# Seven gate chunks of 440 columns in place of six of 512 in a two-block model kernel

## What is computed

```python
h = rmsnorm(x, norm_mix_g[l])
proj = h @ w_in[l]                  # 1024 x 5384
(lru_x, lru_gate, m_qk, m_v, m_o, m_i, m_f,
 s_q, s_k, s_v, g_a, g_b, g_c) = jnp.split(proj, split_points, axis=-1)
...
merged = (jax.nn.sigmoid(g_a) * ya + jax.nn.sigmoid(g_b) * yb
          + jax.nn.sigmoid(g_c) * yc)
x = x + merged @ w_o[l]
```

## Time and profile before

| | us |
|---|---|
| median of three runs | 749.79 |
| lowest and highest of the three | 749.12, 750.28 |
| span of the profiled execution | 748.0 |
| busy: PE, PEld | 740.5, 648.8 |
| busy: DVE, ACT, POOL | 523.8, 402.5, 49.7 |

### The profile page before, as it was taken

One profiled execution on the slowest core, in us unless ns is written; L12 is line 12 of the kernel. 1 busy time (PEld: TensorE's weight loads), 2 busy tenths in 40 slices (PEclk: granted clock), 3 DMA queues, 4 the chain that ended last, 5 costly groups with the idle time before them and its releaser, 6 DMA issues.

```text
span 748.0 us, 10384 instructions
## 1 busy us (share of the span) xinstructions
PE 740.5 (99%) x4280; PEld 648.8 (87%) x4280; DVE 523.8 (70%) x612; ACT 402.5 (54%) x509; POOL 49.7 (7%) x71
## 2 busy tenths in 40 slices
PE   9999999999999999999999999999999999999996
PEld 9988888889988888888899898789988988888885
DVE  6788946885766666656779998785758655556564
ACT  6678378544545545444653685673647443454442
POOL 0200002120000000000230200030003000000000
PEclk9999999999999999999999999999999999999999
DMA  9866365555565556666466536365065466555431
GB/s 337 280 224 225 137 237 210 171 171 168 176 219 169 170 171 204 215 203 209 154 218 205 165 117 225 116 235 165 21 212 166 162 221 225 172 199 188 162 123 57
DMA packets 74239, 138.42 MB, mean 185 GB/s; under 512 B 3916, under 2 KB 28368, under 8 KB 74064
## 3 DMA queue, kind: packets, MB, share of 16 engines
q1 hardware_dynamic: 72336, 132.69, 52.9%
q10 hardware_dynamic: 1856, 5.06, 1.9%
HBM read 136.69 MB, written 1.05 MB: 184 GB/s over the span
## 4 chain that ended last, share of the span: by engine, by line
PE 97%; DVE 2%; issue 0%; ACT 0%; DVEq 0%; ACTq 0%
PE wide L2074 70%; PE bank L2074 25%; PE bank L2198 2%; DVE low L1318 0%; DVE arena L1581 0%; ACT arena L723 0%; DVE act_hl L1415 0%; DVE xn L1809 0%; DVE x L1819 0%; DVE arena L1641 0%; DVE arena L1637 0%; DVE hid_l L1646 0%; DVE arena L1643 0%; DVE arena L1627 0%; DVEq L263 0%
## 5 line engine op out<-in xcount | busy, mean ns | idle before, releaser
L1318 DVE TENSOR_TENSOR low<-raw,high 128x2048 fp32r<-128x2048 f32 (+1 forms) x118 | 267.0, 2279 | 106.2 <-ACT high L723 101.5
L723 ACT ACTIVATE high<-raw 128x2048 fp32r<-128x2048 f32 (+3 forms) x134 | 234.7, 1770 | 122.8 <-PE wide L2074 95.9
L2074 PE MATMUL wide<-act_hl,high 128*128 128x256 f32 (+1 forms) x1184 | 241.3, 327 | 0.0
L2074 PEld LDWEIGHTS wide<-act_hl,high 128*128 128x128 f32 x1184 | 198.9, 191 | 18.3 <-issue 0.2
L2074 PE MATMUL wide<-high,act_hl 128*128 128x512 f32 x528 | 170.1, 394 | 0.5 <-DVE arena L1581 0.2
L2074 PE MATMUL wide<-act_hl,low 128*128 128x256 f32 x832 | 161.2, 284 | 0.0
L2074 PEld LDWEIGHTS wide<-act_hl,low 128*128 128x128 f32 x832 | 128.6, 192 | 2.8 <-DVE low L1366 0.2
L2074 PEld LDWEIGHTS wide<-high,act_hl 128*128 128x128 f32 x528 | 99.1, 188 | 23.3 <-issue 1.7
L2074 PE MATMUL wide<-low,act_hl 128*128 128x512 f32 x264 | 103.0, 390 | 0.0
L2074 PE MATMUL bank<-high,hid_l 128*128 128x512 f32 x216 | 84.4, 391 | 0.3 <-DVE hid_l L1646 0.3
L2074 PE MATMUL bank<-low,hid_h 128*128 128x512 f32 x216 | 84.2, 390 | 0.0
(11 more groups left out here) (215 smaller groups left out, 681.1 us busy)
## 6 DMA issues: line engine op xcount, KB each, us to landing
raw<-in_w_ff_dram SPq DMA_DIRECT2D x32, 1024.0 KB, 5.3
raw<-in_w_in_dram SPq DMA_DIRECT2D x27, 1024.0 KB, 5.3
raw<-in_w_ffn_in_dram SPq DMA_DIRECT2D x44, 512.0 KB, 4.9
raw<-in_w_ffn_out_dram SPq DMA_DIRECT2D x11, 1024.0 KB, 6.5
raw<-in_w_xkv_dram SPq DMA_DIRECT2D x8, 1024.0 KB, 5.0
raw<-in_w_o_dram SPq DMA_DIRECT2D x4, 1024.0 KB, 5.1
raw<-in_w_out_dram SPq DMA_DIRECT2D x4, 1024.0 KB, 5.0
raw<-in_w_xq_dram SPq DMA_DIRECT2D x4, 1024.0 KB, 5.2
```

Source lines behind the costliest of these rows:

```text
L723: return act.activation(dst, src, func, **k)
L1318: tt(part(low, g), part(raw, g), f32(part(high, g)), SUB).then_inc(sem.low_by_dve, 1)
L2074: return pe.matmul(dst, lhs, rhs, start=start, stop=stop, skip_group_check=loose)
```

## The change

The gate columns are cut into chunks of 440 columns instead of 512: seven instead of six, the last one of 432. The groups keep their view of 512 columns by four row tiles, of which 440 are loaded, split and used, so a gate group holds 1,760 numbers per partition instead of 2,048, and there are 14 gate groups instead of 12. Each chunk still takes 48 matmuls, of 440 columns. The hand-written places of the mixers' small matmuls stay at the same chunk numbers and row tiles; the seventh chunk stands behind the sixth on every engine, with a wait on `gate_in` of its own.

```diff
+GATES = 7
+GATE_W = 440
...
+def gate_width(c):
+    return min(GATE_W, 3 * D - c * GATE_W)
...
-    for c in range(6):
-        add(("gate", c), win, 0, KD, [(0, 2312 + c * NB, NB)], NB)
+    for c in range(GATES):
+        add(("gate", c), win, 0, KD, [(0, 2312 + c * GATE_W, gate_width(c))], NB)
...
+                n = gate_width(c)
                 for t, b in enumerate(me.pair()):
-                    f(gates[:, t, c * NB:(c + 1) * NB], b[:, :], ACT.Tanh, scale=half_rstd[:, t:t + 1])\
+                    f(gates[:, t, c * GATE_W:c * GATE_W + n], b[:, 0:n], ACT.Tanh, scale=half_rstd[:, t:t + 1])\
...
             ahead_of_half(("gate", 5), 1)
             gate_in(5)
+            ahead_of(("gate", 6), "T")
+            gate_in(6)
             high_of_branch(2)
...
             ahead_of_half(("gate", 5), 1)
+            ahead_of(("gate", 6), "T")
             low_of_branch(2)
...
-                    pe.wait_ge(sem.gate_in, 12)
+                    pe.wait_ge(sem.gate_in, 2 * GATES)
...
-            products(("gate", 3), "T")
+            products(("gate", 3), "T", width=GATE_W)
             pe.wait_ge(sem.gate_in, 6)
-            products(("gate", 4), "T", at={3: sb_sums})
+            products(("gate", 4), "T", width=GATE_W, at={3: sb_sums})
             sb_out()
             pe.wait_ge(sem.gate_in, 8)
-            products(("gate", 5), "T", at={1: rep_mem})
+            products(("gate", 5), "T", width=GATE_W, at={1: rep_mem})
+            pe.wait_ge(sem.gate_in, 10)
+            products(("gate", 6), "T", width=gate_width(6))
```

More of the change, by code:

```diff
@@ L2536, in _ @@
             pe.wait_ge(sem.vo_in, 2)
-            products(("gate", 0), "T")
+            products(("gate", 0), "T", width=GATE_W)
             pe.wait_ge(sem.sqk_in, 2)
-            products(("gate", 1), "T", at={2: mlstm_scores})
+            products(("gate", 1), "T", width=GATE_W, at={2: mlstm_scores})
             mlstm_out()
             pe.wait_ge(sem.gate_in, 2)
-            products(("gate", 2), "T", at={6: mlstm_turn})
+            products(("gate", 2), "T", width=GATE_W, at={6: mlstm_turn})
             sb_scores()
             pe.wait_ge(sem.gate_in, 4)
-            products(("gate", 3), "T")
+            products(("gate", 3), "T", width=GATE_W)
             pe.wait_ge(sem.gate_in, 6)
-            products(("gate", 4), "T", at={3: sb_sums})
+            products(("gate", 4), "T", width=GATE_W, at={3: sb_sums})
             sb_out()
             pe.wait_ge(sem.gate_in, 8)
-            products(("gate", 5), "T", at={1: rep_mem})
+            products(("gate", 5), "T", width=GATE_W, at={1: rep_mem})
+            pe.wait_ge(sem.gate_in, 10)
+            products(("gate", 6), "T", width=gate_width(6))
             pe.wait_ge(sem.act_hl, me.seen("act_hl", 2))
```

## The result

The changed kernel takes 751.34 us (751.13 to 752.13) beside 749.61 for the kernel before: +1.73 us; the ratio of the runs' means is 1.0026 with an interval of 1.0016 to 1.0035. That is inside the range (749.0 to 751.9), but not the forecast: I had put 750.6 and a time within 0.2%, and it is slower by a little more than that, an outcome that I gave 0.20. The profiled execution's span went from 748.0 to 749.6.

A forecast was written before the change was run, and what follows sets the result against it. PE was taken to bound the kernel, busy 99% of the span; 0 for its matmuls plus 0.81 us of new wait took the median of 749.79 to 750.6, range 749.0 to 751.9.

The forecast's parts named there:

- What bounds the kernel: Whole kernel: PE is busy 99% of the span, so only its matmuls' cost or its waits move the time.
- The price of the matmuls: PE's gate matmuls: cost in proportion to columns, 0.443 ns each, so 336 narrower ones take the same 65.28 us: 0.
- The rival of the fixed price: Gate matmuls: 13.3 ns fixed on each costs 0.64 us, plus 0.62 of wait: +1.26, 751.1; chance 0.13.
- The early arrival and its wait: Chunk 2's end to chunk 5's diagonals: PE comes 3.25 us earlier and newly waits 0.81 us in all (0.5 to 1.2).
- The chain's saving: ACT's and DVE's work from chunk 2 to the diagonals gets 1.38 us shorter through smaller gate operations.
- the room: At chunk 5's diagonals before the change: 1.06 us between the second diagonal, hand-over included, and PE's need of it.
- What had cover: mLSTM's transpose, work queued behind the wait, extra operations, loads and the order behind the gates: no new wait expected.
- the mLSTM's transpose: Small PE step in chunk 2: PE comes 4.2 us earlier, DVE 1.2, and about 1.3 us of room stay.
- the swapped banks: The pair of banks that each later chunk takes is swapped, costed at nothing.
- The rival in which the chain doesn't shrink: ACT's and DVE's gate operations cost as before, so the wait is 2.19 us: 752.0; chance 0.12.
- the steps: Gate matmuls take the next multiple of 32 columns: gain 2.56 us, wait 1.64, in sum -0.9, 748.9; chance 0.10.
- No wait: At the diagonals the chain is looser than its rows look, so the change does nothing: 749.8; chance 0.09.

The follow-up runs named there:

- the streams: Behind the changed kernel's last product, streams of 30 matmuls, one width each from 512 to 256 columns: 226.7 ns each at 512, 200.0 at 440, 119.8 at 256.

## Why the prediction came out as it did

**What bounds the kernel** was right: PE throughout, and the whole change is in PE's gate stage.

**The price of the matmuls was the step that failed.** I took it in proportion to the columns, 0.443 ns each, and so 0; it was +1.73 us. The argument was that the first matmul of 256 columns behind wide ones takes 0.11 us, half of what 512 take. The half was a coincidence: there are 6.7 ns above the columns at 256 (113.3 with 64 or 32 stationary columns) and 13.3 at 512, but 13 to 18.5 from 320 to 504. Neither were my bounds wide enough: at 440 the price, 16.7, is outside both ends (11.5 in proportion, 13.3 fixed). Of the 1.73, 48 x 13.3 ns = 0.64 is for the count and the other 1.09 for the width, some 3.3 ns more at each of 288 and 2.8 at each of 48. The rival of the fixed price, 751.1, was right that a matmul has a price beside its columns, and I gave it 0.13; it had that price too low and the wait too high (0.62), so that its sum, 1.26, came nearer than its terms.

**The early arrival and its wait were right in kind.** With the price that was measured, the forecast's own sum is 102 x 26.7 ns = 2.72 early, less 1.38, less 1.06: 0.28 us of wait; the trace has 0.34. I had forecast 0.81 mostly because I thought PE faster than it is. The chain's saving was 1.38 by my terms; from ACT's read of chunk 2 to the second diagonal it took 126.74 - 98.67 = 28.07 us before and 121.08 - 94.43 = 26.65 after, 1.42 less. That 0.28 lies so near 0.34 is partly luck, because I took the room at the second diagonal, and PE stopped for the first. In the trace of before (timeline of DVE) the first one is done at 126.54:

```profile
126.26 0.28 DVE L1374 TENSOR_SCALAR diag<-ident,rstd 128x128 f32<-128x128 f32 x1
```

The room there is 127.77 - 126.54 - 0.06 = 1.17. From the last matmul of chunk 2 to the place of the product PE takes 127.77 - 98.24 = 29.53 us before and 120.72 - 94.03 = 26.69 after, so it is 2.84 early; the 0.12 more than 2.72 are got back behind the small matmuls. 2.84 - 1.42 - 1.17 leaves 0.25 us, for the 0.23 of the trace, and starting again, which I had only among the bounds, adds 0.11. Low parts of 1,760 elements took 1.98 us for 2.0 expected, so rows of 440 out of 512 carry no price of their own. Lengthening the chain, lengthening PE's lead and moving the product all moved the wait by about what the sum says.

**What I had not seen** is the 0.3 us behind the small matmuls, which the matmuls of 440 columns get back. Why they do wasn't tested.

**What had cover** kept it: no wait at the mLSTM's transpose, on a load, or behind the gates, and the swapped banks cost nothing that shows.

**The sum** had one term at nothing that was 1.73, one that was 0.47 too large, and left out the 0.3: 0.81 + 1.73 - 0.47 - 0.3 gives the 1.78 of the trace; the medians have 1.73. That the time lies in the range is partly luck. With the price put right the forecast's way of adding gives 1.73 + 0.28, 751.8, just below the upper end, which I had set for other reasons; the 0.3 that I had not seen and a median of before that is 749.61 over seven runs instead of 749.79 over three brought it down to 751.34. The rival in which the chain doesn't shrink, 752.0, and the steps, 748.9, are both excluded: by the low parts and by the streams. No wait, 749.8, is excluded by the 0.34.

## What to carry to other kernels

Where TensorE is the bound, as here, cutting the same columns into more chunks cost a price for each matmul, and in these runs the price depended on the width (13 to 18.5 ns from 320 to 512 columns): time a stream of the very width before trusting a line through two others. A hand-written order that ties small products to chunk numbers moves with the chunks; sum how much earlier the engine arrives, how much shorter the other engines' chain gets, and the room, and take the room at the first thing that the engine needs there; the wait came out to a tenth of a microsecond in the three runs that had one.

## What the runs showed of the hardware

In this split-precision form, at full granted clock (1.00), a matmul of 320 to 512 columns with 128 stationary columns takes 0.4167 ns for each column (80.0 ns from 320 to 512) and 13 to 18.5 ns on top; all operands in one place changed that by 0.5 ns at most, and a shift of one by 8 or 16 columns by nothing (200.0 ns at 440, 195.8 at 432). At 400, 440 and 512 columns the price doesn't fall with 64 or 32 stationary columns. With 64 stationary columns a matmul of 128 or 256 takes 60.0 and 113.3 ns, 6.7 above the columns; with 128 stationary columns it takes 111.8 and 119.8. That fits a load that sets the pace there, and these streams don't part it from the smaller result. The price isn't monotonic: 504 columns cost as much as 512 (226.7 ns), and 512 itself takes 230 to 232 ns with 64 or 32 stationary columns and 226.7 with 128. What makes it so stays open.
